# Expert weights in 8 KB runs, an earlier fourth split, and separate buffers for the first item of the expert loop

## The chip, the cores and the metric

One Trainium2 chip, one of its cores. The metric is the device time of one execution in microseconds (us), on the slowest core, which here is the only one. Of the kernel before three executions were timed.

## What is computed

One layer for two groups of tokens (256 prompt and 64 sample tokens, 1024 features, float32): modulation by a condition vector, one wide projection, retention and attention with forget gates, three output projections, a layer norm, a second modulation, and a mixture of 32 experts of which every token visits two. The change touches the second modulation and the mixture:

```python
h = x * (1 + sc2) + sh2                      # after the first layer norm
g_prob = softmax(h @ w_rg + b_rg)            # 4 groups, the best one is taken
e_logits = h @ w_re + b_re                   # 8 experts in the group, the best two
a, u = split(h[t] @ w_e_in[e], 2)            # w_e_in[e] is 1024 x 1024
y = (silu(a) * u) @ w_e_out[e] * gate        # w_e_out[e] is 512 x 1024
```

## The kernel before

The layer ahead of the experts streams 68 blocks of weights, 1 MB each, and ends near 575 us of the span. Then come the second modulation, the router and the sorting of tokens into items, and from about 622 us the loop of experts. An item is one expert with up to 64 token slots; there are 32 items in this run, and all 32 experts' weights are read, 6 MB for each.

**Numbers in two parts.** Products with weights run in TensorE's fp32r form on a high and a low part of each operand. ACT copies a block `raw` (128 x 2048) to its rounded high part `whi` (`item_hi`, L997), DVE subtracts it from the block to get the low part `wlo` (`item_lo`, L1618). There are six raw buffers and three pairs of parts. The last of an item's six blocks is not split: PE reads it from its raw buffer in plain float32 (`product_plain`, L2075).

**One item.** `item_products(e)` on PE multiplies the transposed tokens `xT` with blocks 0 and 1 (L2063 for the high parts, L2067 for the low ones), transposes the hidden rows of the item before (`hidden_T`, L2082), multiplies with blocks 2 and 3, transposes the tokens of the next item (`x_transpose`, L2054), and ends with the second product of the item before: block 4 split, block 5 plain. Its first product goes to banks 0 and 1 of PSUM, the second to banks 2 and 3.

**The order of the work** is written out by hand, one list for each engine. On ACT: split 0, silu of the item before, split 1, `y_low`, split 2, `hidden_high` (L1014), splits 3 and 4, `au_low` (L1018), `x_high` (L1002). On DVE: low part 0, `hidden` (L1631), low 1, `y_sum` (L1642), low 2, `hidden_low` (L1635), lows 3 and 4, `au_sum` (L1627), `x_low` (L1622). A split into slot 0 or 1 for blocks 3 and 4 waits until PE has used blocks 0 and 1 of the same item (`split_free`). SP sends the six blocks in order (L571), each when its raw buffer is free: after its low part is made, or for block 5 after PE has used it. POOL gathers the tokens of an item (L744, L767) and scatters its result (L750, L777).

**Runs of the transfers.** Partition p of a block takes rows p and 128 + p of 256 rows, each 4 KB long, so a block is 256 runs of 4 KB. Token features lie on the partitions in the same order.

**The first item.** Item 0 uses the same `xT` and the same banks 0 and 1 as all others. So the tokens of item 1 are transposed after item 0's four products (`x_transpose(1)`), ACT brings them to `xT` behind `au_low`, and item 1's first product waits for `au_drained`. The last block of item 0 has extra buffers (`xhi`, `xlo`).

**Modulation and router.** `modulated(t)` makes the rows `h2` of 128 (or 64) tokens with two instructions (L1215, L1217); PE transposes them and multiplies with the router weights `wr` (`logits`, L2013). POOL loads `wr` (L722, L723) and stores `h2` for the gathers (L729, L731).

## Time and profile before

| | us |
|---|---|
| median of three executions | 1201.11 |
| lowest, highest | 1198.50, 1202.01 |
| the profiled execution's own time | 1200.38 |
| its span, first to last instruction | 1198.5 |
| mean granted clock of TensorE | 0.942 of full |

| stretch of the span | what it is |
|---|---|
| 0 to 575 us | the layer ahead of the experts |
| 575 to 622 us | second modulation, router, sorting |
| 622 to 649 us | items 0 and 1 |
| 649 to 1141 us | thirty items in a steady rhythm |
| 1141 to 1198.5 us | last product, gathering of the results, second layer norm |

How to read it: the profile is one execution. For each engine it gives busy time, and for each instruction what ended the idle time before it. PE is TensorE, PEld its weight loads, DVE VectorE, ACT ScalarE, POOL GpSimd, SP the engine that only sends transfers. A matmul's duration in the rows overlaps that of the next one; what it costs is seen from start to start. DMA share is how busy the core's 16 DMA engines were; it can pass 1, since a packet's time includes waiting.

### The profile page before, as it was taken

The page shows a single profiled execution, that of the slowest core. Times are in us where ns is not written, and L with a number is a line of the kernel's source. Part 1 is how long each engine was busy: PE and PEld are TensorE (multiplying, and loading weights), DVE is VectorE, ACT ScalarE, POOL GpSimd, SP SyncE. Part 2 cuts the span into 40 slices and gives each one's busy share as a digit, 9 for nine tenths or more (in the row PEclk, how much of TensorE's full clock was granted, in tenths as well). Part 3 has the DMA queues.
Part 4 walks back from the last instruction along what each step waited for, and adds up shares of the span by engine and source line. Part 5 has one row for each costly group of instructions (what it writes and reads, how often), then busy time and mean ns, then how long its engine had stood idle before and what let it go on. Part 6 is the DMA issues. An engine that isn't in the chain of part 4 may idle for free.

```text
span 1198.5 us, 13069 instructions
## 1 busy us (share of the span) xinstructions
PE 1030.9 (86%) x4460; PEld 718.5 (60%) x4460; DVE 882.7 (74%) x942; ACT 638.0 (53%) x646; POOL 198.2 (17%) x179
## 2 busy tenths in 40 slices
PE   4798789899999999999748999999999999999940
PEld 2365567587777677677636566566566566565630
DVE  3768884396433544565857999999999999899967
ACT  3654324223323344433407777777777777777832
POOL 1250671010001000002001221121221121221210
PEclk8788899999999999999758999999999999999975
DMA  9777544265123324336428999999999999999922
GB/s 325 268 264 239 200 151 158 80 214 181 53 80 124 123 79 150 106 141 202 133 88 297 403 394 389 388 392 396 396 393 397 396 395 391 383 392 392 397 76 99
DMA packets 102698, 303.41 MB, mean 253 GB/s; under 512 B 10770, under 2 KB 10818, under 8 KB 102150
## 3 DMA queue, kind: packets, MB, share of 16 engines
q1 hardware_dynamic: 92888, 282.75, 63.5%
q0 software_dynamic: 9776, 20.21, 5.4%
q8 instruction: 21, 0.34, 0.1%
q14 instruction: 13, 0.11, 0.0%
HBM read 299.99 MB, written 14.73 MB: 263 GB/s over the span
## 4 chain that ended last, share of the span: by engine, by line
PE 68%; DVE 15%; ACT 6%; DMA 4%; issue 4%; POOL 2%; SPq 0%; ACTq 0%; POOLq 0%; DVEq 0%
PE banks L2067 10%; PE banks L1753 10%; PE banks L1764 10%; PE banks L2075 8%; PE banks L2063 8%; PE banks L1755 6%; DVE w_lo L1618 6%; ACT w_hi L997 5%; DVE w_lo L1081 3%; PE banks L2054 2%; PE banks L2082 1%; DMA w_raw<-in_w_ada 1%; PE banks L1814 1%; DMA scratch_y<-y_item,slot_row_now 1%; POOL h_hi L644 1%
## 5 line engine op out<-in xcount | busy, mean ns | idle before, releaser
L1618 DVE TENSOR_TENSOR w_lo<-w_raw,w_hi 128x2048 fp32r<-128x2048 f32 x157 | 356.0, 2284 | 47.3 <-ACT w_hi L997 47.3
L997 ACT ACTIVATE w_hi<-w_raw 128x2048 fp32r<-128x2048 f32 x157 | 295.5, 1903 | 7.4 <-PE banks L2067 7.2
L1081 DVE TENSOR_TENSOR w_lo<-w_raw,w_hi 128x2048 fp32r<-128x2048 f32 x71 | 170.3, 2413 | 69.8 <-ACT w_hi L815 69.7
L815 ACT ACTIVATE w_hi<-w_raw 128x2048 fp32r<-128x2048 f32 x71 | 134.8, 1910 | 133.2 <-PE banks L1764 108.4
L2067 PE MATMUL banks<-w_lo,xT_item 128*128 128x512 f32 x508 | 147.5, 412 | 41.3 <-DVE w_lo L1618 41.3
L2063 PE MATMUL banks<-w_hi,xT_item 128*128 128x512 f32 x508 | 157.1, 432 | 4.1 <-DVE xT_item L1622 3.6
L1753 PE MATMUL banks<-w_hi,h_hi 128*128 128x512 f32 x384 | 141.0, 408 | 7.9 <-DVE mod_rows L1237 5.2
L2067 PEld LDWEIGHTS banks<-w_lo,xT_item 128*128 128x128 f32 x508 | 91.9, 190 | 85.9 <-DVE w_lo L1618 68.0
L2063 PEld LDWEIGHTS banks<-w_hi,xT_item 128*128 128x128 f32 x508 | 94.6, 192 | 39.3 <-issue 14.3
L2075 PE MATMUL banks<-w_raw,hiddenT 128*128 128x512 f32 x248 | 111.5, 592 | 0.0
L1764 PE MATMUL banks<-w_lo,h_hi 128*128 128x512 f32 x384 | 108.5, 404 | 3.3 <-DVE w_lo L1081 3.3
L1755 PE MATMUL banks<-w_hi,h_lo 128*128 128x512 f32 x256 | 102.2, 399 | 0.0
L750 POOL DMA_INDIRECT scratch_y<-y_item,slot_row x29 | 63.2, 2179 | 234.1 <-DVE y_item L1642 217.6
L1753 PEld LDWEIGHTS banks<-w_hi,h_hi 128*128 128x128 f32 x384 | 72.0, 189 | 27.3 <-issue 6.0
L1764 PEld LDWEIGHTS banks<-w_lo,h_hi 128*128 128x128 f32 x384 | 69.8, 189 | 20.9 <-DVE w_lo L1081 3.7
L2075 PEld LDWEIGHTS banks<-w_raw,hiddenT 128*128 128x128 f32 x248 | 47.2, 190 | 47.4 <-issue 44.5
L1018 ACT ACTIVATE au_low<-banks 64x1024 f32<-64x1024 f32 x32 | 32.8, 1025 | 58.0 <-PE banks L2067 58.0
L744 POOL DMA_INDIRECT x_item<-scratch_h,slot_token x32 | 30.2, 943 | 195.8 <-PE banks L2054 174.9
L1755 PEld LDWEIGHTS banks<-w_hi,h_lo 128*128 128x128 f32 x256 | 48.7, 190 | 10.4
L1415 DVE TENSOR_REDUCE neg_max<-banks 64x1 f32<-64x192 f32 x16 | 5.6, 350 | 62.4 <-PE banks L1935 62.4
L1010 ACT ACTIVATE y_low<-banks 64x1024 f32<-64x1024 f32 x32 | 32.8, 1025 | 25.5 <-PE banks L2075 17.4
L1804 PE MATMUL banks<-w_lo,c_parts 128*64 128x512 f32 x96 | 34.4, 492 | 13.5 <-DVE w_lo L1081 13.1
(431 smaller groups left out, 1444.3 us busy)
## 6 DMA issues: line engine op xcount, KB each, us to landing
w_raw<-in_w_e_in SPq DMA_DIRECT2D x128, 1024.0 KB, 7.3
w_raw<-in_w_e_out SPq DMA_DIRECT2D x64, 1024.0 KB, 6.6
w_raw<-in_w_in SPq DMA_DIRECT2D x32, 1024.0 KB, 7.9
w_raw<-in_w_ada SPq DMA_DIRECT2D x24, 1024.0 KB, 7.7
bias_rows<-in_b_in SPq DMA_DIRECT2D x16, 256.0 KB, 4.3
w_raw<-in_w_ret_proj SPq DMA_DIRECT2D x4, 1024.0 KB, 10.6
w_raw<-in_w_fox_proj SPq DMA_DIRECT2D x4, 1024.0 KB, 11.6
w_raw<-in_w_o SPq DMA_DIRECT2D x4, 1024.0 KB, 5.0
```

Of the source, the lines that this page charges most:

```text
L750: nc.gpsimd.indirect_dma_start(yd[:, :], bass.IndirectOffsetOnAxis(ap=row[:, e:e + 1], axis=0), ySb[:].rearrange("p a b -> p (a b)"), None ...
L815: nc.scalar.activation(whi[n % NSPL][:], raw[n % NRAW][:], ACT.Copy).then_inc(hi_done, 1)
L997: nc.scalar.activation(whi[ss][:], raw[j][:], ACT.Copy).then_inc(hi_done, 1)
L1081: V.tensor_tensor(wlo[n % NSPL][:], raw[n % NRAW][:], whi[n % NSPL][:].bitcast(F32), ALU.subtract).then_inc(lo_done, 1)
L1618: V.tensor_tensor(wlo[ss][:], raw[j][:], whi[ss][:].bitcast(F32), ALU.subtract).then_inc(lo_done, 1)
L1753: mm(b[:, :], H[:, k, cols], whi[n % NSPL][:, kk, :], start=(k == 0), stop=False)
L1755: mm(b[:, :], L[:, k, cols], whi[n % NSPL][:, kk, :], start=False, stop=False)
L1764: last = mm(b[:, :], H[:, 4 * s + kk, P * t:P * t + P], wlo[n % NSPL][:, kk, :], start=False, stop=(s == 1 and kk == 3))
L1804: last = mm(b[0:64, :], cst[:, 4 * s + kk, :], wlo[n % NSPL][:, kk, :], start=False, stop=(s == 1 and kk == 3))
L2063: mm(bank[b0 + half], X[:, k0 + kk, :], split_h[ss][:, 2 * kk + half, :], start=(first and kk == 0), stop=False)
L2067: last = mm(bank[b0 + half], X[:, k0 + kk, :], split_l[ss][:, 2 * kk + half, :], start=False, stop=(final and kk == 1))
L2075: last = mm(bank[b0 + half], X[:, k0 + kk, :].bitcast(F32), raw[rs][:, 2 * kk + half, :], start=False, stop=(kk == 1))
```

## The change

**Rows of the weights.** Partition p of a block now takes rows 2p and 2p + 1 of 256 rows. They lie side by side in memory, so a block is 128 runs of 8 KB. To match, feature 256j + 2p + i has to stand in the place 256j + 128i + p. `modulated` writes `h2` in that order, with four instructions in place of two, each reading every second element; `hidden` writes the hidden rows so, in one instruction that reads every second element; the router weights are loaded in that order by four transfers in place of two, and two waits count 96 in place of 64.

**Order of the fourth split.** On ACT split 3 comes ahead of `hidden_high`, on DVE low part 3 ahead of `hidden_low`, in every item.

**First item.** Item 0 has its own `xT0` and banks 6 and 7. Item 1's tokens are transposed after item 0's second product, brought to `xT` ahead of `au_low`, and item 1's first product no longer waits for `au_drained`. PE waits for the drained banks 6 and 7 before item 0.

**POOL** waits for item 0's four products before it sends the six transfers for the tail (L783 to L788).

```diff
+    xT0 = at("xT_first", [P, KD, 2 * SLOTS], F32R, 73728)
...
-    w_in_e = i["w_e_in"][0].rearrange("e (k p) n -> e p k n", p=P)
-    w_out_e = i["w_e_out"][0].rearrange("e (k p) n -> e p k n", p=P)
+    w_in_e = i["w_e_in"][0].rearrange("e (j p i) n -> e j p (i n)", p=P, i=2)
+    w_out_e = i["w_e_out"][0].rearrange("e (j p i) n -> e j p (i n)", p=P, i=2)
...
+    FIRST_BANK = 6
 
     def sub(e, j):
 
...
                 sp.dma_start(bf_col[:], i["b_in"][0, FGATE:FGATE + FH].rearrange("(p a) -> p a", a=1)).then_inc(wf_in, 16)
 
         def pair(r):
-            return r[:].rearrange("p a b -> p (a b)").rearrange("p (k n) -> p k n", k=2)
+            return r[:].rearrange("p a b -> p (a b)")
 
         for n in range(4):
             s = N0 + n
             sp.wait_ge(lo_done, s - NRAW + 1)
-            sp.dma_start(pair(raw[s % NRAW]), w_in_e[0, :, 2 * n:2 * n + 2, :]).then_inc(raw_landed[s % NRAW], 16)
+            sp.dma_start(pair(raw[s % NRAW]), w_in_e[0, n]).then_inc(raw_landed[s % NRAW], 16)
 
         def raw_free(e, j):
 
...
             for j in range(6):
-                src = (w_in_e[expert, :, 2 * j:2 * j + 2, :] if j < 4
-                       else w_out_e[before, :, 2 * (j - 4):2 * (j - 4) + 2, :])
+                src = w_in_e[expert, j] if j < 4 else w_out_e[before, j - 4]
                 if not isinstance(e, int):
-                    src = src.rearrange("e p k n -> (e p) k n")
+                    src = src.rearrange("e p n -> (e p) n")
                 raw_free(e, j)
                 sp.dma_start(pair(raw[j]), src).then_inc(raw_landed[j], 16)
...
-        pool.dma_start(wr[:, :, 0:NG], i["w_rg"][0].rearrange("(k p) n -> p k n", p=P)).then_inc(wr_in, 16)
-        pool.dma_start(wr[:, :, NG:], i["w_re"][0].rearrange("(k p) n -> p k n", p=P)).then_inc(wr_in, 16)
+        wr4 = wr[:].rearrange("p (j i) n -> p j i n", i=2)
+        for half in range(2):
+            pool.dma_start(wr4[:, :, half, 0:NG], i["w_rg"][0].rearrange("(j p i) n -> p j i n", p=P, i=2)[:, :, half, :]).then_inc(wr_in, 16)
+            pool.dma_start(wr4[:, :, half, NG:], i["w_re"][0].rearrange("(j p i) n -> p j i n", p=P, i=2)[:, :, half, :]).then_inc(wr_in, 16)
         pool.dma_start(br[:, 0:NG], bcast(i["b_rg"][0], P)).then_inc(wr_in, 16)
         pool.dma_start(br[:, NG:], bcast(i["b_re"][0], P)).then_inc(wr_in, 16)
 
...
         gather_item(1)
         gather_item(2)
+        pool.wait_ge(used, N0 + 4)
         pool.dma_start(g2p[:], bcast(md[0, 3 * D:4 * D], P)).then_inc(tail_in, 16)
         pool.dma_start(g2s[:], bcast(md[1, 3 * D:4 * D], DEC)).then_inc(tail_in, 16)
         pool.dma_start(l1w[:], bcast(i["ln1_w"][0], P)).then_inc(tail_in, 16)
...
             act.wait_ge(x_trans, e + 1)
-            nc.scalar.activation(xT[:, :, 0:SLOTS], bank[4][:, :].rearrange("p (k c) -> p k c", k=KD), ACT.Copy).then_inc(x_hi, 1)
+            dst = xT0 if isinstance(e, int) and e == 0 else xT
+            nc.scalar.activation(dst[:, :, 0:SLOTS], bank[4][:, :].rearrange("p (k c) -> p k c", k=KD), ACT.Copy).then_inc(x_hi, 1)
 
...
             act.wait_ge(used, after + 1)
-            nc.scalar.activation(auLo[:], banks[SLOTS:P, 0:2, :], ACT.Copy).then_inc(au_lo, 1)
+            b0 = FIRST_BANK if isinstance(after, int) and after == N0 + 3 else 0
+            nc.scalar.activation(auLo[:], banks[SLOTS:P, b0:b0 + 2, :], ACT.Copy).then_inc(au_lo, 1)
 
         x_high(0)
         item_hi(1, 0)
+        x_high(1)
         au_low(N0 + 3)
-        x_high(1)
 
         def item(e, second):
             if not (isinstance(e, int) and e == 1):
...
                 y_low(e - 2, sub(e - 1, 5))
             item_hi(e, 2)
+            item_hi(e, 3)
             hidden_high(e - 1)
-            item_hi(e, 3)
             item_hi(e, 4)
             au_low(sub(e, 3))
             x_high(e + 1)
...
-            st(V.scalar_tensor_tensor(ht, xt, mv[0:rows, t, 0:1], m2[0:rows, 1, :], ALU.subtract, ALU.mult))
-            st.settle()
-            st(V.scalar_tensor_tensor(ht, ht, mv[0:rows, t, 1:2], m2[0:rows, 0, :], ALU.mult, ALU.add), h2_ready)
+            for i in range(2):
+                hv = ht.rearrange("r (j i p) -> r j i p", i=2, p=P)[:, :, i, :]
+                st(V.scalar_tensor_tensor(hv, xt.rearrange("r (j p i) -> r j p i", i=2, p=P)[:, :, :, i], mv[0:rows, t, 0:1],
+                                          m2[0:rows, 1, :].rearrange("r (j p i) -> r j p i", i=2, p=P)[:, :, :, i], ALU.subtract, ALU.mult))
+            st.settle()
+            for i in range(2):
+                hv = ht.rearrange("r (j i p) -> r j i p", i=2, p=P)[:, :, i, :]
+                st(V.scalar_tensor_tensor(hv, hv, mv[0:rows, t, 1:2], m2[0:rows, 0, :].rearrange("r (j p i) -> r j p i", i=2, p=P)[:, :, :, i],
+                                          ALU.mult, ALU.add), h2_ready if i else None)
 
         def evac_ada(j):
...
             dve.wait_ge(x_hi, e + 1)
-            V.tensor_tensor(xT[:, :, SLOTS:], bank[4][:, :].rearrange("p (k c) -> p k c", k=KD),
-                            xT[:, :, 0:SLOTS].bitcast(F32), ALU.subtract).then_inc(x_split, 1)
+            dst = xT0 if isinstance(e, int) and e == 0 else xT
+            V.tensor_tensor(dst[:, :, SLOTS:], bank[4][:, :].rearrange("p (k c) -> p k c", k=KD),
+                            dst[:, :, 0:SLOTS].bitcast(F32), ALU.subtract).then_inc(x_split, 1)
 
...
-            V.tensor_tensor(auS[:], banks[0:SLOTS, 0:2, :], auLo[:], ALU.add).then_inc(au_drained, 1)
+            b0 = FIRST_BANK if isinstance(e, int) and e == 0 else 0
+            V.tensor_tensor(auS[:], banks[0:SLOTS, b0:b0 + 2, :], auLo[:], ALU.add).then_inc(au_drained, 1)
 
         def hidden(e):
             dve.wait_ge(silu_ok, e + 1)
-            V.tensor_tensor(hid[:], aA[:], auS[:, 1, :], ALU.mult).then_inc(hid_ok, 1)
+            V.tensor_tensor(hid[:].rearrange("r (j i p) -> r j i p", i=2, p=P), aA[:].rearrange("r (j p i) -> r j i p", i=2, p=P),
+                            auS[:, 1, :].rearrange("r (j p i) -> r j i p", i=2, p=P), ALU.mult).then_inc(hid_ok, 1)
 
         def hidden_low(e):
...
         dve.wait_ge(hi_done, N0 + 4)
         V.tensor_tensor(xlo[:], raw[(N0 + 3) % NRAW][:], xhi[:].bitcast(F32), ALU.subtract).then_inc(lo_done, 1)
         x_low(0)
+        x_low(1)
         item_lo(1, 0)
         au_sum(0)
-        x_low(1)
 
...
                 y_sum(e - 2, third)
             item_lo(e, 2)
+            item_lo(e, 3)
             hidden_low(e - 1)
-            item_lo(e, 3)
             item_lo(e, 4)
...
         x_transpose(0)
         pe.wait_ge(x_split, 1)
         pe.wait_ge(slt_done, 1)
+        pe.wait_ge(*use["pos"][3])
+        pe.wait_ge(*use["cnt"][3])
         for n in range(4):
-            product(N0 + n, (N0 + n) % NSPL if n < 3 else NSPL, 0, xT, 2 * n, n == 0, n == 3)
-        x_transpose(1)
+            product(N0 + n, (N0 + n) % NSPL if n < 3 else NSPL, FIRST_BANK, xT0, 2 * n, n == 0, n == 3)
+            if n == 1:
+                x_transpose(1)
 
         def item_products(e, second):
             pe.wait_ge(x_split, e + 1)
-            pe.wait_ge(au_drained, e)
+            if not (isinstance(e, int) and e == 1):
+                pe.wait_ge(au_drained, e)
             for j in range(2):
                 product(split_sub(e, j), SPLIT_SLOT[j], 0, xT, 2 * j, j == 0, False)
```

## Rows read from the trace of the kernel before

**Rows 1.** Windows: us, busy us of each engine, clock, DMA share, GB/s; the loop

```profile
700.00:1100.00 400.00, 367.76 (x1507) 242.61 (x1506) 366.73 (x245) 306.52 (x245) 75.10 (x49) 1.00 1.01 392
```

**Rows 2.** Waits of ACT in the loop, and issue to landing of two items' weights

```profile
ACT w_hi L997 <- PE banks L2067: 0.4, 1, 0.4
...
w_raw<-in_w_e_in SPq DMA_DIRECT2D x8, 1024.0 KB, 7.5
```

**Rows 3.** Timeline of one item, DVE: start, us, instruction, idle before and its releaser

```profile
907.09 4.49 DVE L1618 TENSOR_TENSOR w_lo<-w_raw,w_hi 128x2048 fp32r<-128x2048 f32 x2 [0.56 <-ACT w_hi L997]
...
914.14 2.29 DVE L1618 TENSOR_TENSOR w_lo<-w_raw,w_hi 128x2048 fp32r<-128x2048 f32 x1 [0.61 <-ACT w_hi L997]
...
920.29 2.27 DVE L1618 TENSOR_TENSOR w_lo<-w_raw,w_hi 128x2048 fp32r<-128x2048 f32 x1
922.49 0.41 DVE L1635 TENSOR_TENSOR hiddenT<-banks,hiddenT 128x256 fp32r<-128x256 f32 x1
923.46 2.29 DVE L1618 TENSOR_TENSOR w_lo<-w_raw,w_hi 128x2048 fp32r<-128x2048 f32 x1 [0.56 <-ACT w_hi L997]
```

**Rows 4.** The same item's timeline, ACT and PE

```profile
912.21 1.91 ACT L997 ACTIVATE w_hi<-w_raw 128x2048 fp32r<-128x2048 f32 x1
...
917.89 1.91 ACT L997 ACTIVATE w_hi<-w_raw 128x2048 fp32r<-128x2048 f32 x1
921.24 0.39 ACT L1014 ACTIVATE hiddenT<-banks 128x256 fp32r<-128x256 f32 x1 [1.44 <-PE banks L2082]
921.52 3.71 ACT L997 ACTIVATE w_hi<-w_raw 128x2048 fp32r<-128x2048 f32 x2
...
909.44 1.19 PE L2067 MATMUL banks<-w_lo,xT_item 128*128 128x512 f32 x4 [1.06 <-DVE w_lo L1618]
...
917.69 1.10 PE L2067 MATMUL banks<-w_lo,xT_item 128*128 128x512 f32 x4
```

**Rows 5.** Token transposes that bound thirty items, from the PE timeline

```profile
648.55 0.62 PE L2054 MATMUL banks<-pack,x_item 64*128 64x64 f32 x5
...
1141.29 0.87 PE L2054 MATMUL banks<-pack,x_item 64*128 64x64 f32 x9
```

**Rows 6.** DMA of 900 to 934 us, then windows with 2 KB, 4 KB and 8 KB runs

```profile
DMA packets 3747, 13.43 MB, mean 395 GB/s; under 512 B 469, under 2 KB 469, under 8 KB 3746
...
20.00:30.00 10.00, 7.17 (x20) 3.53 (x20) 5.95 (x4) 3.82 (x2) 0.00 (x0) 0.66 1.05 387
904.00:916.00 12.00, 10.65 (x47) 6.82 (x46) 10.70 (x7) 9.30 (x8) 3.13 (x2) 1.00 1.03 412
...
1167.00:1171.00 4.00, 0.00 (x0) 0.00 (x0) 0.52 (x3) 1.15 (x1) 0.00 (x0) 0.50 1.01 426
```

**Rows 7.** Window of the loop in which the granted clock fell

```profile
1026.00:1029.00 3.00, 3.00 (x8) 2.33 (x9) 2.26 (x4) 2.98 (x4) 0.94 (x1) 0.52 1.03 416
```

**Rows 8.** DVE groups by shape: hidden, the modulation, two reductions

```profile
L1631 DVE TENSOR_TENSOR hidden<-a_silu,au_sum 64x512 f32<-64x512 f32 x32 | 21.6, 676 | 0.8 <-ACT a_silu L1006 0.8
...
L1217 DVE SCALAR_TENSOR_TENSOR h<-h,ln_mean_var,mod_prompt 128x1024 f32<-128x1024 f32 x2 | 2.6, 1285 | 0.1
...
L1515 DVE TENSOR_REDUCE expert_logits<-expert_masked 128x24 f32<-128x96 f32 x1 | 0.3, 322 | 0.0
...
L1554 DVE TENSOR_REDUCE extra_items<-count_cmp 128x32 f32<-128x128 f32 x1 | 0.3, 285 | 0.0
```

**Rows 9.** Timeline of items 0 and 1, ACT

```profile
632.13 1.02 ACT L1018 ACTIVATE au_low<-banks 64x1024 f32<-64x1024 f32 x1 [1.73 <-PE banks L2067]
633.18 0.60 ACT L1002 ACTIVATE xT_item<-banks 128x512 fp32r<-128x512 f32 x1
...
635.62 3.70 ACT L997 ACTIVATE w_hi<-w_raw 128x2048 fp32r<-128x2048 f32 x2
```

**Rows 10.** POOL's loads of the router weights

```profile
564.18 0.94 POOL L722 DMA_DIRECT2D w_router<-in_w_rg  x1 [8.57 <-PE banks L1764]
...
587.53 3.60 PE L2013 MATMUL banks<-w_router,h2T 128*128 128x36 f32 x16 [0.78 <-ACT h2T L972]
```

6 lines of the change are left out of this document (3 added, 3 removed).

## The prediction

> **What bounds the kernel now.** I read the loop first, since thirty items of it take 492.74 us of the span: the token transposes at both ends of it start at 648.55 and 1141.29 [rows 5], so an item takes 16.42 us in the mean. The windows then show three resources near their end at once: over 400 us PE is busy for 92%, DVE for 92%, and the DMA engines for all of it at 392 GB/s [rows 1]. A busy share doesn't say which one sets the pace, so I look at waits. ACT, the first to touch a block of weights, never waits for a transfer in the loop; its one wait ahead of a split is 0.4 us for PE [rows 2]. So the transfers keep up, and DMA is full because SP sends early. What sets the pace is a ring of hand-overs. Follow DVE: it idles twice in an item, 0.61 us ahead of low part 0 and 0.56 us ahead of low part 3, both times for a split on ACT [rows 3]. ACT makes split 3 late because it stands behind `hidden_high`, for which ACT sat idle for 1.44 us until PE had transposed the hidden rows [rows 4]. PE in turn waits 1.06 us for low part 3 [rows 4]. From low part 3 to the next low part 3 an item takes 923.46 - 907.09 = 16.37 us [rows 3].
>
> **The fourth split.** The ring in two parts. From low part 3 to low part 0 it is 914.14 - 907.09 = 7.05 us [rows 3]: low part 3, PE's last four matmuls at 909.44, `au_low`, `x_high`, split 0 at 912.21 for 1.91 us [rows 4]. Nothing in it moves. `hidden_low` now lies between low parts 3 and 4, which ends 0.41 us later; low part 3 itself is not moved by that, and of the 0.61 us that DVE idles ahead of low part 0 some 0.1 goes, since `au_sum` now comes behind low part 4 and not behind `au_low`. It still waits for split 0.
>
> From low part 0 to low part 3 it was 923.46 - 914.14 = 9.32 us. Low part 3 now stands where `hidden_low` starts, right behind low part 2, at 922.49 [rows 3]. That takes off 0.97 us: 0.56 of idle and 0.41 of `hidden_low`, which lands where DVE had idle time. The ring is then 922.49 - 907.09 = 15.40 us.
>
> What could be late next, each by the same timeline. Split 3 follows split 2: 917.89 + 2 x 1.86 = 921.6 (two splits in a row take 3.71), 0.9 us ahead of its low part [rows 4]. It needs the slot of block 0, which PE leaves at 917.69 + 1.10 = 918.79, 0.9 us before ACT asks for it at 919.7 [rows 4]. `hidden_high` moves from 921.24 to 921.6, split 4 behind it to about 921.9 and ends by 923.8; low part 4 wants it at 922.49 + 2.20 + 0.33 = 925.0, so 1.2 us are spare. `hidden_low` starts behind low part 3, near 924.7, and PE wants it after its token transpose, two microseconds after low part 3: spare. On PE the pause of 1.06 us ahead of low part 3 shrinks to about 0.1.
>
> Thirty items: 492.74 - 30 x 15.40 = 30.7 us. Of this 29.1 are the ring and 1.6 the one item above 16.37: from 1026 to 1029 PE's clock was granted at 0.52 of full speed, that is its lower level of 1.2 GHz, where the loop as a whole shows 1.00, the higher one of 2.4 GHz [rows 1, 7]. PE had not done less before it than in every item: it had made its pause ahead of low part 3. With shorter pauses I take this one as gone; if it stays, 1.6 us are to be added.
>
> **8 KB runs.** An item moves 13.43 MB x 16.37 / 34 = 6.47 MB [rows 6]. Where DMA is full, 2 KB runs went at 387 GB/s, 4 KB runs, which this loop has, at 412, and the one transfer with 8 KB runs, the gathering of results at the end, at 426 over 4 us [rows 6]. The steps 387 and 412 give the same by a fixed cost for each run: on one of 16 engines 2 KB takes 84.7 ns and 4 KB 159.1 ns, so another 4 KB 148.8, and 8 KB in 308 ns on 16 engines are 426 GB/s. An item then needs 6.47 / 0.426 = 15.19 us of DMA, under the 15.40 of the ring; with 4 KB runs it would be 15.70, over it. So the longer runs are worth nothing alone (DMA is hidden now), and make room for the other part. I take 15.19, with 15.70 as the upper end. Landing: low part 0 is made at 916.43 and the next split 0 starts 16.37 after 912.21, at 928.58; a block lands 7.5 us after it is sent [rows 2]. At most 4.6 us are spare for SP's own delay, 3.7 after the change: enough.
>
> The Trainium skill (DMA: Bandwidth & Descriptors, Why small descriptors are slow) puts a packet's own cost at some 3 beats beside one for each 32 bytes. By it 8 KB runs would be 1.2% faster than 4 KB ones, 417 GB/s and 15.5 us for an item, 0.1 us above the ring. The trace shows 6.5% between 2 and 4 KB where that rule gives 2.3%, so it doesn't agree.
>
> **Reading every second element.** `hidden` (676 ns) lies on the ring, between low parts 0 and 1 [rows 8]. No row reads 512 elements at this step. From below the cost is nothing. From above I take the one row that reads at a wide step, a reduction of 96 elements over steps of 8: 322 ns, where 128 elements in a row took 285 [rows 8]. An element costs 1.19 ns (1285 - 676 ns for 512 more, the two shapes of [rows 8]), so 96 in a row would take 247; the step costs 75 ns, 0.78 for an element, and on 512 that is 0.40 us for an item. I take nothing, since the step is two and that row's is eight, and keep 0.40 for the range. The modulation pays the same on its 1285 ns instructions [rows 8], of which only the first tokens' two stand before anything can hide them: split in four they add some 0.1 us, for two more starts, and 4 x 0.4 = 1.6 us at the upper end.
>
> The Trainium skill (SBUF — State Buffer, Door 1) says that SBUF is read in lines of 16 bytes and that two hits on a line are enough for full speed. Every second float32 gives two hits, every eighth one; the row with the step of eight agrees with it. By this rule `hidden` keeps its 676 ns.
>
> **The first item.** The transpose of item 1's tokens now lies between item 0's products: 9 small matmuls of 0.87 us together [rows 5], so `au_low` moves from 632.13 to about 633.0. `x_high` of 0.60 us no longer stands between it and the table load that silu needs, and split 1 of item 1, which leads the chain from there, moves by 0.87 - 0.60 from 635.62 to 635.9 [rows 9]. PE starts item 1 some 2 us earlier and then waits for that split. I take 0.3 us lost; if PE's clock happens to stay up, up to 3 us are won. POOL's new wait has the tail's six loads and the gather for item 3 queued behind it; the loads are used after the loop, and the gather waits for a later transpose of PE anyway. The two added loads of router weights cost POOL 2 x 0.94 us near 566; with the 7.5 us to land of [rows 2] they are in by 576, and PE wants them at 587.5 [rows 10]. The new waits for banks 6 and 7 are for work long done.
>
> **The sum.** -30.7 + 0.3 + 0.1 = -30.3 us. Against the profiled execution's 1200.38 that is 1170.1; the median of 1201.11 is 0.7 above it, so 1170.8.
>
> **Rivals.**
> - DMA becomes the bound, because 8 KB runs bring nothing: 30 x (16.42 - 15.70) = 21.7, and some 2 us more from buffers that run dry at the end; 1177. For it: only 4 us of trace have 8 KB runs, and they have no gathers beside them. Against it: the two other run lengths point to the same 426. A rate in between gives a time in between.
> - The step of two costs 0.40 us in `hidden`, and 1.6 us in the modulation: 30.3 - 12.0 - 1.6 = 16.7; 1184.4. Only one row, with another step and another instruction, speaks for it.
> - Slower: 8 KB runs go at a lower rate beside gathers, and ACT waits for landings. The point is 6.47 / 16.42 = 394 GB/s. At the 387 of 2 KB runs an item takes 16.72 us; 30 x 0.3 = 9 us more, 1210. Against it: the rate rises with the run in all three rows.
> - The order does not do what it says: the wait for PE only moves from split 3 to split 4 and on to low part 4. It needs more than the 1.2 us that I find spare, plus 0.97; about 1200.
>
> **How the numbers follow.** The ring 0.60, with its own range of 1167 to 1175 (the clock either way, the start); DMA as the bound 0.20; the step of two 0.10; no change 0.04; slower 0.05; better than the ring's range 0.01. The range from 1166 to 1185 holds all but the last three, and I keep these ends since DMA and the step can each be paid in part. A measurement of this kernel can tell about 0.3%, 3.6 us, from no change. Faster 0.91, within 0.3% 0.04, slower 0.05.
>
> **What the profile will show.** Right: low part 3 to low part 3 in 15.4 us; `hidden_low` behind low part 3 with no idle before it; DVE's only idle time in an item ahead of low part 0; PE's pause ahead of low part 3 gone; packets of 8 KB with DMA near 420 GB/s; `hidden` at 676 ns. If splits on ACT show a wait for `w_raw` transfers, DMA is the bound. If `hidden` shows about 1.08 us, the step is paid. If `hidden` is as it was, no transfer is waited for and an item still takes over 16 us, my ring is wrong.

## The result and the profile after

The changed kernel takes 1186.56 us (median of four runs, 1186.50 to 1187.36) against 1201.56 (four runs, 1198.50 to 1205.24): a ratio of 0.9886, 95% interval 0.9856 to 0.9917. So it is faster, by 15.0 us, about half of the 30.3 that were forecast, and the time lies 1.6 us above the forecast's range. The profiled execution took 1186.54 us, its span is 1184.7, and the mean clock 0.944 of full.

Three token transposes of the changed kernel, from the PE timeline (start us, us, instruction), answer to [rows 5]; they open items 2, 10 and the last product. Under them stands the window of the loop that answers to [rows 1]:

```profile
651.40 0.87 PE L2069 MATMUL banks<-pack,x_item 64*128 64x64 f32 x9
775.15 0.87 PE L2069 MATMUL banks<-pack,x_item 64*128 64x64 f32 x9
1127.48 0.87 PE L2069 MATMUL banks<-pack,x_item 64*128 64x64 f32 x9
...
700.00:1100.00 400.00, 382.04 (x1559) 248.44 (x1558) 374.46 (x253) 327.94 (x252) 113.00 (x51) 1.00 1.01 406
```

Thirty items now take 1127.48 - 651.40 = 476.08 us, 16.66 less than the 492.74 of before. But they are of two kinds. The first eight take (775.15 - 651.40) / 8 = 15.47 us, six of them 15.38 to 15.40, which is the ring of 15.40 that was forecast. The other 22 take (1127.48 - 775.15) / 22 = 16.01 us. Both kinds can be read in DVE's timeline, first an item at 682, then one at 907:

```profile
686.05 2.29 DVE L1630 TENSOR_TENSOR w_lo<-w_raw,w_hi 128x2048 fp32r<-128x2048 f32 x1 [0.51 <-ACT w_hi L1001]
688.25 0.68 DVE L1645 TENSOR_TENSOR hidden<-a_silu,au_sum 64x512 f32<-64x512 f32 x1
...
691.06 1.21 DVE L1657 TENSOR_TENSOR y_item<-banks,y_low 64x1024 f32<-64x1024 f32 x1
692.19 4.48 DVE L1630 TENSOR_TENSOR w_lo<-w_raw,w_hi 128x2048 fp32r<-128x2048 f32 x2
696.59 0.41 DVE L1650 TENSOR_TENSOR hiddenT<-banks,hiddenT 128x256 fp32r<-128x256 f32 x1
...
907.43 2.29 DVE L1630 TENSOR_TENSOR w_lo<-w_raw,w_hi 128x2048 fp32r<-128x2048 f32 x1 [1.35 <-ACT w_hi L1001]
...
923.58 2.29 DVE L1630 TENSOR_TENSOR w_lo<-w_raw,w_hi 128x2048 fp32r<-128x2048 f32 x1 [1.20 <-ACT w_hi L1001]
```

Against [rows 3], low part 3 stands behind low part 2 (the `x2` at 692.19), `hidden_low` follows with no idle time, and the only idle time of the item at 682 is the one ahead of low part 0. In the later item this same idle time has grown from 0.51 to 1.35 us. DVE waits there for split 0, and ACT's timeline says what split 0 waits for:

```profile
904.16 0.60 ACT L1007 ACTIVATE xT_item<-banks 128x512 fp32r<-128x512 f32 x1
905.49 1.91 ACT L1001 ACTIVATE w_hi<-w_raw 128x2048 fp32r<-128x2048 f32 x1 [0.73 <-DMA w_raw<-in_w_e_in]
...
911.54 1.91 ACT L1001 ACTIVATE w_hi<-w_raw 128x2048 fp32r<-128x2048 f32 x1 [0.63 <-DMA w_raw<-in_w_e_in]
```

Now the loop's waits (engine and line, what it waited for: us in total, times, longest) and the landing of the weights from 900 to 934 us (KB each, us from issue to landing), which answer to [rows 2]:

```profile
ACT w_hi L1001 <- DMA w_raw<-in_w_e_in: 26.8, 57, 1.0
DVE w_lo L1630 <- ACT w_hi L1001: 25.0, 29, 1.4
...
w_raw<-in_w_e_in SPq DMA_DIRECT2D x8, 1024.0 KB, 11.3
```

Before, ACT waited for no transfer of weights in the loop and a block landed 7.5 us after it was sent. Now it waits 57 times for one, and a block takes 11.3 us. So the ring was shortened as forecast, and from about the eighth item on the transfers set the pace, at 16.0 us for an item where the forecast had 15.19. The change from one kind to the other shows in the time from issue to landing, here from 650 to 680 us and from 740 to 770 us:

```profile
w_raw<-in_w_e_in SPq DMA_DIRECT2D x7, 1024.0 KB, 7.6
...
w_raw<-in_w_e_in SPq DMA_DIRECT2D x8, 1024.0 KB, 10.8
```

The transfers of 900 to 934 us in 40 equal slices, and two windows (us, busy us of each engine, clock, DMA share, GB/s), answer to [rows 6]:

```profile
GB/s 414 424 395 381 410 424 434 443 414 414 414 280 318 405 424 405 443 414 424 414 443 405 419 400 434 376 453 434 414 424 313 304 318 434 443 376 443 443 424 376
DMA packets 2152, 13.75 MB, mean 404 GB/s; under 512 B 422, under 2 KB 422, under 8 KB 526
...
912.00:919.00 7.00, 6.01 (x26) 3.93 (x25) 7.00 (x6) 5.68 (x4) 1.96 (x1) 1.00 1.01 419
909.00:911.50 2.50, 2.50 (x11) 1.88 (x10) 2.50 (x3) 1.89 (x2) 0.00 (x0) 1.00 1.02 326
```

The packets fell from 3747 to 2152, so the 8 KB runs are there, and in most slices they go at 400 to 440 GB/s. But once per item the rate falls to about 300 for some 2.5 us, with the DMA engines as busy as before. POOL's timeline has the gather of an item's tokens at 904.65 and 920.97; it lands 7.3 us after it is sent. What these dips are is the question of the experiments.

### The profile page after: what moved, and what is told of

Its sections match the earlier page's. It is cut to its first block, busy times and chain, and to the rows that moved or that the text cites. A ratio compares the mean times of both kernels' runs of the same rounds, so it can differ in the third digit from the quotient of the medians.

```text
span 1184.7 us, 13078 instructions
## 1 busy us (share of the span) xinstructions
PE 1033.2 (87%) x4460; PEld 716.2 (60%) x4460; DVE 878.8 (74%) x948; ACT 651.5 (55%) x646; POOL 257.7 (22%) x181
## 4 chain that ended last, share of the span: by engine, by line
PE 47%; DVE 20%; DMA 15%; issue 10%; ACT 5%; POOL 2%; SPq 1%; ACTq 0%; POOLq 0%; DVEq 0%
PE banks L1768 10%; PE banks L1779 10%; DMA w_raw<-in_w_e_in 10%; DVE w_lo L1630 9%; PE banks L1770 7%; PE banks L2082 3%; ACT w_hi L1001 3%; PE banks L2090 3%; DVE w_lo L1087 3%; PE banks L2078 2%; DMA w_raw<-in_w_ada 1%; DVE y_item L1657 1%; PE banks L1829 1%; POOL h_hi L645 1%; DMA scratch_y<-y_item,slot_row 1%
## 5 line engine op out<-in xcount | busy, mean ns | idle before, releaser
L1001 ACT ACTIVATE w_hi<-w_raw 128x2048 fp32r<-128x2048 f32 x157 | 299.6, 1912 | 44.1 <-DMA w_raw<-in_w_e_in 28.9
L753 POOL DMA_INDIRECT scratch_y<-y_item,slot_row x29 | 113.8, 3925 | 238.7 <-DVE y_item L1657 221.2
L2078 PE MATMUL banks<-w_hi,xT_item 128*128 128x512 f32 x496 | 151.9, 428 | 2.9 <-ACT w_hi L1001 2.9
L2082 PEld LDWEIGHTS banks<-w_lo,xT_item 128*128 128x128 f32 x496 | 87.7, 190 | 72.1 <-DVE w_lo L1630 57.2
L2078 PEld LDWEIGHTS banks<-w_hi,xT_item 128*128 128x128 f32 x496 | 91.6, 190 | 36.5 <-issue 14.3
L1819 PE MATMUL banks<-w_lo,c_parts 128*64 128x512 f32 x96 | 32.1, 464 | 15.6 <-DVE w_lo L1087 15.1
L1816 PE MATMUL banks<-w_hi,c_parts 128*64 128x512 f32 x96 | 32.9, 475 | 13.3 <-ACT w_hi L819 13.3
```

Of the source, the lines that this page charges most:

```text
L753: nc.gpsimd.indirect_dma_start(yd[:, :], bass.IndirectOffsetOnAxis(ap=row[:, e:e + 1], axis=0), ySb[:].rearrange("p a b -> p (a b)"), None ...
L1001: nc.scalar.activation(whi[ss][:], raw[j][:], ACT.Copy).then_inc(hi_done, 1)
L1816: mm(b[0:64, :], cst[:, 4 * s + kk, :], whi[n % NSPL][:, kk, :], start=(s == 0 and kk == 0), stop=False)
L2078: mm(bank[b0 + half], X[:, k0 + kk, :], split_h[ss][:, 2 * kk + half, :], start=(first and kk == 0), stop=False)
L2082: last = mm(bank[b0 + half], X[:, k0 + kk, :], split_l[ss][:, 2 * kk + half, :], start=False, stop=(final and kk == 1))
```

## The experiments

An item's time below is from one token transpose to the next. For each run I compare it with the changed kernel's two values, 15.39 (ring) and 16.02 us (mean of the last twenty).

**The new order alone**, 4 KB runs, first item as before:

```diff
             item_hi(e, 2)
+            item_hi(e, 3)
             hidden_high(e - 1)
-            item_hi(e, 3)
...
             item_lo(e, 2)
+            item_lo(e, 3)
             hidden_low(e - 1)
-            item_lo(e, 3)
```

> The kernel before with split 3 ahead of hidden_high and low part 3 ahead of hidden_low, nothing else: 4 KB runs, the first item as before. Theory A (DMA sets the pace, and longer runs raise its rate): the first items take 15.4 us, then ACT waits for transfers and an item takes 16.2 to 16.4 us; 1194 to 1200 us. Theory B (DMA sets the pace, run length does not matter): items settle at 16.0 us as in the changed kernel; 1186 to 1188 us. My forecast's own rates (4 KB at 412 GB/s): 15.7 us for an item, 1178 us.

Measured: 1193.22 us, ratio 0.9931 (0.9908 to 0.9954). The loop's first two items take 16.14 and 17.04 us, the next two 15.46 and 15.41, then they settle near 16.3 (the last twenty have a mean of 16.35). The loop's window and, of 800 to 1100 us, ACT's wait:

```profile
700.00:1100.00 400.00, 375.02 (x1523) 242.41 (x1522) 366.86 (x246) 322.13 (x246) 87.83 (x49) 1.00 1.02 398
...
ACT w_hi L997 <- DMA w_raw<-in_w_e_in: 23.0, 37, 1.0
```

The order works by itself, and with 4 KB runs the transfers allow 398 GB/s and 16.35 us. That is nearly the old ring of 16.37, so before the change two bounds lay on top of each other. Not all of the 8.6 us is the order's. The loop of the profiled execution gains 4.2 us (488.52 against 492.74). Another 2.8 lie in items 0 and 1, which take 26.12 us from the first to the third token transpose where they took 28.92. The granted clock is what differs there: it fell near 640 us in the kernel before, and not in this execution. The windows from 640 to 649 us, before and here:

```profile
640.00:649.00 9.00, 9.00 (x30) 6.54 (x31) 6.69 (x4) 4.33 (x4) 0.00 (x0) 0.62 1.02 350
```

```profile
640.00:649.00 9.00, 9.00 (x45) 6.58 (x45) 8.33 (x6) 6.51 (x6) 0.98 (x1) 1.00 1.02 351
```

In the changed kernel it fell there too (0.65 in the same window), so this gain does not come with the order.

**The longer runs alone**, with the old order and the old first item:

```diff
-            item_hi(e, 3)
             hidden_high(e - 1)
+            item_hi(e, 3)
...
-            item_lo(e, 3)
             hidden_low(e - 1)
+            item_lo(e, 3)
```

(against the changed kernel; its first item is undone too, as in the run on the first item below)

> The changed kernel with the old order of the fourth split and the old first item; only the 8 KB runs and the permuted rows are left. All theories: the old ring sets the pace with 16.37 us for an item, ACT never waits for a transfer; 1199 to 1202 us. If the ring was not what held the kernel before and DMA was, it drops to 16.0 us and 1188 us.

Measured: 1202.62 us, ratio 1.0012 (0.9984 to 1.0040). Items take 16.37 us, and ACT has no wait for a transfer. The window of its loop and the landing of its weights:

```profile
700.00:1100.00 400.00, 368.05 (x1497) 242.86 (x1496) 363.94 (x243) 304.08 (x243) 76.39 (x49) 0.99 0.98 390
...
w_raw<-in_w_e_in SPq DMA_DIRECT2D x8, 1024.0 KB, 7.0
```

The runs are worth nothing alone, as forecast. The DMA share is 0.98 here, where before it was 1.01 with 4 KB runs and the same 16.37 us.

**What the transfers allow.** The changed kernel with half of each low part left out (the subtraction of blocks 0 to 4 covers half a block), once with 8 KB and once with 4 KB runs. That takes some 5 us of DVE from an item, so DVE no longer sets the pace:

```diff
-            V.tensor_tensor(wlo[ss][:], raw[j][:], whi[ss][:].bitcast(F32), ALU.subtract).then_inc(lo_done, 1)
+            V.tensor_tensor(wlo[ss][:, 0:2, :], raw[j][:, 0:2, :], whi[ss][:, 0:2, :].bitcast(F32), ALU.subtract).then_inc(lo_done, 1)
```

> The changed kernel with every low part of the loop's blocks made for half of the block only (the other half keeps old numbers, so part of the products is left wrong): DVE's ring falls well under 15 us and the pace is that of the transfers alone. Theories A and B: 16.0 us for an item, about 404 GB/s, ACT waiting for weights in every item, near 1184 to 1187 us. My forecast's rate of 426 GB/s: 15.2 us for an item, 1163 us.

> The same with the 4 KB runs and the old order of features: half low parts, pace of the transfers alone. Theory A: 16.2 to 16.4 us for an item, 395 to 399 GB/s. Theory B: 16.0 us. My forecast's rate of 412 GB/s: 15.7 us.

Measured: 1183.60 us with 8 KB runs, ratio 0.9848 (0.9783 to 0.9913), and 1192.99 with 4 KB, ratio 0.9927 (0.9893 to 0.9962). Both begin with items of 14.5 us: three with 8 KB runs, two with 4 KB. Then 8 KB runs give 16.00 and 4 KB runs 16.35 us (last twenty). The two windows of the loop, 8 KB first:

```profile
700.00:1100.00 400.00, 388.97 (x1554) 245.41 (x1553) 247.90 (x251) 328.36 (x251) 47.94 (x50) 1.00 1.01 407
```

```profile
700.00:1100.00 400.00, 385.99 (x1519) 237.70 (x1517) 242.80 (x245) 321.73 (x245) 50.84 (x49) 1.00 1.02 398
```

DVE, the third engine of the window, has 248 busy us instead of 374, and an item takes what it takes in the changed kernel (16.00 against 16.02). That is the floor of the transfers. Doubling the run is worth 0.35 us in an item, 2.1%. The Trainium skill (DMA: Bandwidth & Descriptors, Why small descriptors are slow) has a fixed cost for each packet, from which an estimate of 1.2% follows for this step. These runs show more than that, and less than the 3.4% that the forecast took from short windows.

**Gathers that move nothing.** The row numbers of all gathers from item 1 on are out of range, so that they are sent and land but move no token. The items then work on item 0's tokens, with the same instructions:

```diff
-        st(V.tensor_copy(idx[:], slt[:, 0, :]), idx_ready)
+        st(V.tensor_scalar(idx[:, 1:], slt[:, 0, 1:], SKIP, None, ALU.add))
+        st(V.tensor_copy(idx[:, 0:1], slt[:, 0, 0:1]), idx_ready)
```

> The changed kernel with the gathers of items 1 and up pointed out of range, so that they move no token rows (all items then work on item 0's tokens; the output is not the layer's). Once in an item the rate of all transfers falls to 326 GB/s for 2.5 us while the gather's rows move. Theory C (the gather slows all transfers, beyond its own 0.08 MB): the dips are gone, the floor falls to about 6.37 MB at 419 GB/s = 15.2 us, the ring of 15.4 us sets the pace, ACT's waits for transfers vanish; 1172 to 1176 us. Theory D (the dip has another cause that only falls together with the gather): 15.8 us for an item by the bytes saved, 1181 to 1184 us.

Measured: 1174.01 us, ratio 0.9761 (0.9718 to 0.9804). The first item of the loop takes 15.69 us and the other 29 take 15.38 to 15.40 to the end, ACT waits for no transfer in the loop, and a block lands in 8.3 us. The DMA share of the loop is still 1.01, at 414 GB/s, though no engine waits for a transfer. The transfers of 900 to 934 us, as above:

```profile
GB/s 414 434 424 424 386 443 419 400 434 386 366 405 424 395 405 434 443 414 414 424 453 424 395 443 400 410 434 405 357 405 453 395 414 424 443 424 434 395 443 424
DMA packets 2236, 14.17 MB, mean 417 GB/s; under 512 B 482, under 2 KB 482, under 8 KB 532
```

The dips are gone, while the scatters of results are still there. So the dips belong to the rows that the gathers bring, and they are what keeps the changed kernel from its ring: 16.02 - 15.39 = 0.63 us for an item at the least. A gather brings 20 rows of 4 KB in the mean (640 visits in 32 items), 0.08 MB, which at 417 GB/s would be 0.2 us. The changed kernel's window of the dip gives the same size: 2.5 x (419 - 326) / 419 = 0.55 us. Without them the kernel is 2.4% faster than the one before, 28.7 us of 1202.8 (1174.01 / 0.9761), close to the 30.3 forecast.

**Where the rows come from.** Gathers from item 1 on read the same row numbers of another tensor, `w_o`; the items work on those rows:

```diff
...
-            nc.gpsimd.indirect_dma_start(xg[:], None, h2d[:, :], bass.IndirectOffsetOnAxis(ap=idx1[:, 0:1], axis=0),
+            nc.gpsimd.indirect_dma_start(xg[:], None, other[:, :], bass.IndirectOffsetOnAxis(ap=idx1[:, 0:1], axis=0),
```

> The changed kernel with the gathers of items 1 and up reading the same row numbers of another tensor of 4 KB rows (w_o) in place of the stored h2 (output not the layer's). If it matters where the rows lie in memory, the dips go and an item takes 15.4 to 15.6 us. If the dip belongs to the gather as such, whatever it reads: 16.0 us for an item, 1186 to 1188 us.

Measured: 1185.42 us, ratio 0.9856 (0.9812 to 0.9900), items of 16.05 us, and the dips as before. It makes no difference which of these two tensors the rows come from.

**Where the rows go.** The tokens of an item are spread, with a step of four partitions. 20 tokens then lie on partitions 0 to 31 instead of 0 to 19 (slots from 32 on go to partitions 32 to 63 in the same way); all is computed:

```diff
-        st(V.tensor_tensor(oh_s[:], io_s, cp6.unsqueeze(2).to_broadcast([P, 6, SLOTS]), ALU.is_equal))
+        for g in range(2):
+            cols = slice(32 * g, 32 * g + 32)
+            st(V.tensor_tensor(oh_s[:, :, cols].rearrange("p q (a b) -> p q b a", b=4),
+                               iota[:, cols].rearrange("p (b a) -> p b a", a=8).unsqueeze(1).to_broadcast([P, 6, 4, 8]),
+                               cp6.unsqueeze(2).unsqueeze(3).to_broadcast([P, 6, 4, 8]), ALU.is_equal))
```

> The changed kernel with the slots of an item permuted over the 64 partitions, so that the first 8 tokens lie 4 partitions apart instead of side by side; everything is still computed. Theory E (the gather's rows fall on few partitions, whose share of the engines' paths is loaded more than the others): the dips get shorter, an item takes 15.7 to 15.9 us, 1178 to 1184 us. Otherwise 16.0 us, 1186 to 1188 us.

Measured: 1186.02 us, ratio 0.9852 (0.9815 to 0.9888); items of 15.91 us instead of 16.02. In the time no difference to the changed kernel can be told. The items are 0.1 us shorter, a little more than the changed kernel's own traces differ (15.98 to 16.02 in three of them). The crowding is only lessened by this run and not removed; what 0.1 us means is taken up below.

**The first item as before**, with the new runs and the new order:

```diff
-            dst = xT0 if isinstance(e, int) and e == 0 else xT
+            dst = xT
...
-        x_high(1)
         au_low(N0 + 3)
+        x_high(1)
...
-            product(N0 + n, (N0 + n) % NSPL if n < 3 else NSPL, FIRST_BANK, xT0, 2 * n, n == 0, n == 3)
-            if n == 1:
-                x_transpose(1)
+            product(N0 + n, (N0 + n) % NSPL if n < 3 else NSPL, 0, xT, 2 * n, n == 0, n == 3)
+        x_transpose(1)
```

> The changed kernel with the first item as before (xT, banks 0 and 1, item 1's tokens transposed behind item 0, no new wait on POOL). My forecast and all theories: items as in the changed kernel, 15.4 us for the first and 16.0 us later; the first item's own part is worth 0.3 us or less either way, unless TensorE's clock differs; 1184 to 1188 us.

Measured: 1186.51 us, ratio 0.9876 (0.9838 to 0.9914), the time of the changed kernel. Item 0's own buffers bring nothing and cost nothing that can be told. From the first to the third token transpose it takes 28.8 us, against 29.1 with the buffers and 28.9 before.

**A plain load in the gather's place.** From item 1 on, POOL sends a plain load of stored tokens 0 to 19 (in a second run 0 to 63) instead of the gather, at the same place; all those items work on these tokens:

```diff
...
-            nc.gpsimd.indirect_dma_start(xg[:], None, h2d[:, :], bass.IndirectOffsetOnAxis(ap=idx1[:, 0:1], axis=0),
-                                         bounds_check=T - 1, oob_is_err=False).then_inc(x_landed, 16)
+            pool.dma_start(xg[0:20, :], h2d[0:20, :]).then_inc(x_landed, 16)
```

> The changed kernel, with the gather of every item from item 1 on replaced by one plain load of the rows 0 to 19 of the stored tokens into the same buffer, on the same queue and at the same place. 20 rows of 4 KB are what a gather moves in the mean (640 token visits over 32 items), to the same partitions 0 to 19. All these items then work on the same 20 tokens; the sequence of instructions on the other engines is unchanged. Theory F, it is the indirect form that costs (a row address for every packet, made on the way): the items after the first seven fall to 15.4 to 15.5 us and the time to about 1174 to 1176 us, as with gathers that moved no rows (1174.0). Theory G, it is any small load in packets of 4 KB into few partitions beside the stream of weights: the items stay near 16.0 us and the time near 1186. A plain load might be cut into other packets than a gather; the packets show it.

> As the run before, with rows 0 to 63 in the plain load: 0.26 MB on 64 partitions, 0.18 MB more than 20 rows. At the 407 GB/s of the stream that alone is 0.45 us of transfer time for an item. Theory F: items of 15.4 (the ring) plus at most that, since the ring has 0.2 to 0.4 us of spare transfer time; 15.5 to 15.9 us, 1176 to 1184. Theory G: if the cost goes with the number of small packets, it is three times that of 20 rows: 16.0 + 1.2 = over 17 us, 1220 or more; if it goes with the load as an event, some 16.3 us, 1196.

Measured: 1186.87 us with 20 rows, ratio 0.9863 (0.9806 to 0.9919), items of 15.93 us; 1218.35 with 64 rows, ratio 1.0124 (1.0067 to 1.0182), items of 17.07. The transfers of 900 to 934 us with 64 rows:

```profile
GB/s 405 395 448 434 414 424 424 361 251 284 299 405 405 443 414 414 414 453 405 424 405 414 443 395 443 434 410 294 299 260 308 424 424 405 434 424 424 405 443 405
...
x_item<-scratch_h POOLq DMA_DIRECT2D x2, 256.0 KB, 7.4
```

The indirect form is not the cause: 20 rows by a plain load cost about as much as a gather. By these two, 64 rows make an item at least 17.07 - 15.39 = 1.68 us longer, 26 ns a row, and 20 rows 15.93 - 15.39 = 0.54 us, 27 ns a row, where 4 KB in the stream of weights take 4096 / 417 = 10 ns. That looked like a price for each row.

**The same loads on ACT's queue**, sent behind `x_high`:

```diff
...
-            nc.gpsimd.indirect_dma_start(xg[:], None, h2d[:, :], bass.IndirectOffsetOnAxis(ap=idx1[:, 0:1], axis=0),
-                                         bounds_check=T - 1, oob_is_err=False).then_inc(x_landed, 16)
...
             nc.scalar.activation(dst[:, :, 0:SLOTS], bank[4][:, :].rearrange("p (k c) -> p k c", k=KD), ACT.Copy).then_inc(x_hi, 1)
+            act.dma_start(xg[0:20, :], scratch["h2"][0:20, :]).then_inc(x_land2, 16)
```

(against the changed kernel)

> The run with 20 plain rows, with the load sent by ACT behind the copy of the transposed tokens (`x_high`) instead of by POOL after the same transpose: the same bytes, the same 20 partitions and nearly the same moment, but on ACT's queue, which the hardware serves, and not on POOL's. The send itself stands on ACT's way to split 0, so the ring grows by what it costs ACT; I take 0.1 us (a send of POOL's stands at 0.94 us in the rows, as the upper end). All items work on the same 20 tokens. Theory H, POOL's queue is what makes small packets dear: items after the first eight at the ring, 15.4 to 15.6 us, and 1175 to 1180 us. Theory G, it is the small packets themselves, whoever sends them: near 16.0 us, 1187, as with POOL's load (1186.9).

> The same with 64 rows, 0.26 MB. By POOL's queue the items stood at 17.07 us and the time was 1218. Theory H: a load of 0.26 MB at the stream's rate adds 0.45 us over that of 20 rows, so items of 15.5 to 15.9 us and 1177 to 1187 us. Theory G: as by POOL's queue, items near 17.1 us, 1218.

Measured: 1187.77 us with 20 rows, ratio 0.9858 (0.9752 to 0.9965), last items of 15.91 us, and 1217.50 with 64 rows, ratio 1.0105 (0.9997 to 1.0213), items of 16.97. POOL's queue is not the cause either.

**Is it the rows or where they land?** Two plain loads by POOL from item 3 on, into a spare buffer: 4 rows into partitions 0 to 3, or 64 rows into partitions 32 to 95. Items 1 and 2 load 20 rows, and all items work on those tokens:

```diff
...
-            nc.gpsimd.indirect_dma_start(xg[:], None, h2d[:, :], bass.IndirectOffsetOnAxis(ap=idx1[:, 0:1], axis=0),
-                                         bounds_check=T - 1, oob_is_err=False).then_inc(x_landed, 16)
+            pool.dma_start(xd[0:4, :], h2d[0:4, :]).then_inc(x_landed, 16)
```

> The changed kernel; in place of the gathers from item 3 on POOL sends a plain load of 4 stored rows, 16 KB, into partitions 0 to 3 of a spare buffer (items 1 and 2 load 20 rows). All items from the first on work on the same 20 tokens. Theory R, a price for each row (27 ns by the loads of 20 and 64 rows): 4 rows cost 0.1 us, items at the ring, 15.4 us, and some 1174 us. Theory S, the busiest group of partitions sets the price: partition p belongs to group (p / 4) mod 8 of the lower or upper 64, so partitions 0 to 3 are one group and get 4 rows, as each of the five groups of a load of 20 rows does. The stream's 417 GB/s are 26 GB/s for each of 16 groups; 16 KB more in one of them take 0.63 us. So 4 rows cost what 20 cost: items of 15.9 to 16.0 us, 1186 us. In between would say that the hold-up is shared. The Trainium skill (SBUF — State Buffer, Door 1: The DMA port swizzle) gives this grouping, 16 ports of 8 partitions; the trace so far has nothing against it, since the loads of 20 and of 64 rows cost 0.54 and 1.68 us.

> As the run before, with 64 rows into partitions 32 to 95 of the spare buffer. The same load into partitions 0 to 63 gave items of 17.07 us and 1218 us. Theory R: the same again, 17.0 to 17.1 us and 1218. Theory S: partitions 32 to 63 are eight groups, 64 to 95 the other eight, so each of 16 groups gets 4 rows where partitions 0 to 63 gave each of eight groups 8 rows: the cost is that of one group's 4 rows, 0.63 us, and since all groups are loaded alike it is also just that of the bytes, 0.26 MB at 417 GB/s: items of 15.9 to 16.1 us and 1184 to 1190 us. By the Trainium skill (SBUF — State Buffer, Door 1: The DMA port swizzle) partitions 0 to 63 reach only 8 of 16 ports and 32 to 95 all of them.

Measured: 4 rows 1182.20 us, ratio 0.9833 (0.9787 to 0.9879), items of 15.86 us; 64 rows 1185.38 us, ratio 0.9860 (0.9817 to 0.9902), items of 15.88. The transfers of 900 to 934 us, first with 4 rows (busy tenths of the DMA engines and GB/s in 40 slices), then with 64:

```profile
DMA  9999999899999989999999999999999999899999
GB/s 395 434 434 443 414 395 434 357 453 453 405 405 424 424 308 386 405 424 395 434 414 453 405 405 395 453 386 424 443 386 424 414 347 308 347 366 376 395 424 434
```

```profile
GB/s 434 405 434 414 400 439 424 414 434 405 424 443 395 434 376 395 386 434 453 414 395 434 434 434 395 434 414 434 386 434 453 395 424 414 424 376 434 424 434 405
DMA packets 2172, 14.22 MB, mean 418 GB/s; under 512 B 347, under 2 KB 347, under 8 KB 525
```

A price for each row is out. Against the ring of 15.39, so at the least, 4 rows cost 0.47 us of an item, 20 cost 0.54, and 64 cost 0.49 or 1.68, by where they land. With 64 rows over partitions 32 to 95 there is no dip, and the engines move 418 GB/s in the mean; by this that load costs its bytes (0.26 MB, 0.63 us at 417 GB/s) and no more. With 4 rows in partitions 0 to 3, 16 KB in all, there are dips (308, then 347, 308 and 347 GB/s), and the three slices in which the DMA engines are not fully busy have 357, 308 and 347 GB/s. So for plain loads the cost goes with the rows in the busiest of 16 groups of partitions: 4, 4 and 4 rows in it at 0.47 to 0.54 us, 8 rows at 1.68. A fixed price for any load that brings rows would give the first three too, but neither the 1.68 us nor the missing dip. The forecast for 4 rows was 0.63; for 8 rows the same sum gives 1.26, and the rest of the 1.68 is not explained. The two loads of 64 rows differ in their buffer as well (the spare one against that of the tokens), which was not tried apart; in neither run does an engine wait for the load in the loop. It would fit that a block of weights lands only when its last part has, so that what one group takes on top holds up the whole stream; no view shows the groups one by one. The Trainium skill gives this grouping (SBUF — State Buffer, Door 1: The DMA port swizzle): 16 ports, partitions 0 to 63 reach only 8 of them, and partitions 32 to 95 all. These two runs agree with it. It also says (DMA: Bandwidth & Descriptors, The descriptor swizzle) that in a transfer to all 128 partitions each DMA engine serves one port; whether here the port or its engine is the narrow place no run shows.

**The gather over 16 groups.** First the direct way, with everything computed. Slots go to partitions 0 to 31 and 64 to 95, so that 20 tokens put at most 2 rows in any group; the transposes become plain products with columns of the identity:

```diff
...
-    xg = at("x_item", [SLOTS, D], F32, 0)
+    xg = at("x_item", [96, D], F32, 0)
...
-                step = tr if k else mm
-                last = step(bank[4][:, SLOTS * k:SLOTS * k + SLOTS], xg[:, P * k:P * k + P], ident[0:SLOTS, 0:SLOTS])
+                step = mm
+                last = step(bank[4][:, SLOTS * k:SLOTS * k + SLOTS], xg[:, P * k:P * k + P],
+                            ident[0:96, :].rearrange("q (h x c w) -> q h x w c", h=2, x=2, c=8)[:, :, 0].rearrange("q h w c -> q w h c"))
```

> The changed kernel with everything computed, its gathers spread over all 16 groups of partitions: slot s of an item goes to partition 64h + 4c + w with s = 16w + 8h + c, so that the first 16 tokens go to 16 different groups and 20 tokens put at most 2 rows in any. The buffer has 96 partitions, the token transposes multiply with the matching columns of the identity, and a second small product makes the row numbers for 96 partitions (six matmuls and three instructions more ahead of the first item, some 0.7 us). Theory S: the busiest group gets 2 rows, 8 KB, where it got 4; the load costs 0.2 to 0.32 us of an item where it cost 0.63, and an item takes 15.6 to 15.75 us where it took 16.02; over 22 items 6 to 9 us less, and against the changed kernel 1178 to 1181 us. Theory R: items as before, 16.0, and 1187 to 1188 us. Against both: the gather has 96 row numbers instead of 64, and the transposes as plain products may take PE a little longer, 0.1 us an item on the ring.

> The changed kernel itself, on the same chip and in the same rounds as the run before, so that the two can be compared: 1186 to 1187 us, ratio 0.987 to 0.989.

Measured: 1203.35 us (the median of twelve, of which one took 2556.2), ratio 1.0013 (0.9994 to 1.0031), the loop's first item 16.73 us and all others 16.19; the changed kernel beside it 1183.97, ratio 0.9859 (0.9831 to 0.9887). ACT has no wait for a transfer in the loop; it waits for PE, whose transposes take 2 us where they took 0.87. PE's and ACT's timelines at one of them:

```profile
915.39 2.01 PE L2083 MATMUL banks<-pack,x_item 96*128 96x64 f32 x16
...
917.43 0.60 ACT L1009 ACTIVATE xT_item<-banks 128x512 fp32r<-128x512 f32 x1 [0.82 <-PE banks L2083]
```

Those 0.82 us lie on the ring: 15.39 + 0.82 = 16.21. So the run cannot show a gain, but it sets a limit. The transfers keep up with 16.19 us for an item, and from 900 to 934 us a block lands nearly as soon as in the kernel before (7.5 us):

```profile
w_raw<-in_w_e_in SPq DMA_DIRECT2D x8, 1024.0 KB, 7.8
```

With this gather their floor is thus 16.19 us or less.

Then with true transposes over 96 partitions, into banks 6 and 7, the first item as before the change, and the slots of the scatter spread as well:

```diff
...
-                last = step(bank[4][:, SLOTS * k:SLOTS * k + SLOTS], xg[:, P * k:P * k + P], ident[0:SLOTS, 0:SLOTS])
+                last = step(bank[6 + k // 4][:, P * (k % 4):P * (k % 4) + 96], xg[:, P * k:P * k + P], ident[0:96, 0:96])
```

> The changed kernel with the gathers over 16 groups of partitions and everything computed, as in e15, but with the transposes in transpose mode: 96 columns each, into banks 6 and 7, from which ACT and DVE read the 64 that hold slots. Since items use banks 6 and 7 so, the first item is done as before the change (worth nothing by e8). Ahead of the loop six small products and six DVE instructions more, some 1 us. The ring: eight transposes of 96 instead of 64 columns, of whose 0.87 us `au_low` (1.02) covers all; 0 to 0.3 us more, so 15.4 to 15.7 us. Theory S: the transfers need 15.6 to 15.75 us by the busiest group's 2 rows (0.2 to 0.32 us over the 15.4 that they need at most without rows), so items of 15.6 to 15.8, against 16.0 of the changed kernel, and 22 x 0.25 to 0.4 less 1 us: 1179 to 1183 where the changed kernel of the same rounds has 1184 to 1187. If ACT waits for transfers as before and an item takes 16.0, theory S has no use here. If ACT waits for PE ahead of `x_high`, the transposes are again the price.

> The changed kernel in the same rounds as the run before: 1184 to 1187 us, items of 15.38 to 15.40 and later 16.0 us.

Measured: 1197.68 us, ratio 0.9968 (0.9951 to 0.9986), beside 1185.82, ratio 0.9876 (0.9853 to 0.9899), of the changed kernel. The transposes take 0.94 us, and early items stand at 15.4 to 15.6 us, so the ring is short. But the last twenty take 16.38, more than the changed kernel's 16.01, and ACT waits for transfers more (700 to 1100 us); the rates of 900 to 934 us stand below:

```profile
ACT w_hi L1002 <- DMA w_raw<-in_w_e_in: 35.5, 52, 1.8
...
GB/s 318 337 357 328 376 424 386 434 443 434 386 424 381 434 429 424 410 347 309 328 313 376 357 395 424 414 424 443 414 386 429 429 414 434 434 424 424 333 362 366
```

The dips are longer, not shorter. With 2 rows in the busiest group the forecast was an item of 15.6 to 15.8 us, so here it fails, by some 0.6 us. The 16.38 cannot be the price of the spread gather alone, since the run before had the same gather and a floor of 16.19 or less. The two runs differ in the scatter's slots, the banks and the first item, and in that the transfers bind in one and the ring in the other; which of these counts was not tried.

The run with the step of four partitions does not speak against the groups. 20 tokens put 3 rows in the busiest of 8 groups there and not 4, which by the same sum takes 0.16 us off an item, and 0.11 was measured. So for gathers the groups are neither shown nor out. How a gather's rows are shared out among the DMA engines no view here shows, and this stays open. So does whether two loads per item, or a scatter that moves nothing, would change it; neither was tried. No version of these beats the changed kernel.

## Why the prediction was right in kind and twice too large

**Right: what bounds the kernel before.** The ring of hand-overs by way of low part 3 set the pace. Its length was forecast at 15.40 us from [rows 3], and the trace has 15.38 to 15.40 wherever transfers don't bind: in six early items of the changed kernel, and in 29 of thirty with gathers that move nothing. In the item at 682 us its signs are there: `hidden_low` at once behind low part 3, DVE's only idle time ahead of low part 0, and no pause of PE ahead of low part 3. But the ring was only just the longer of the two. The transfers need 16.35 us for an item in 4 KB runs, and the ring took 16.37; "so the transfers keep up" was true with 0.02 us to spare, which the prediction did not see. In the changed kernel the ring, to which the forecast gave 0.60, sets the pace for some eight items and the transfers for the other 22.

**Right: the runs alone are worth nothing**, and make room for the order: 0.35 us in an item once both are in.

**Wrong: the term for the transfers.** The step that failed is "an item then needs 6.47 / 0.426 = 15.19 us", and with it the upper end of 15.70 for 4 KB runs. The floors are 16.00 and 16.35 us. The bytes were right; the rates were read from windows of 12 and of 4 us in which the rate was high [rows 6]. The window of 12 us lay between two gathers, and that of 4 us stands behind the loop, where no tokens are gathered. Yet the same rows have 395 GB/s over 34 us, and [rows 1] 392 over 400 us at a DMA share of 1.01. At that mean an item needs 6.47 / 0.395 to 6.47 / 0.392, that is 16.4 to 16.5 us. This sum only gives the item's own time back, whatever bounds it. What hinted that it was the transfers' floor too is the share: with 8 KB runs and the old order, where the floor is 16.00 and the ring 16.37, it is 0.98. The hint is a weak one, since the share is also 1.01 with gathers that move nothing, where the ring sets the pace. What shows the floor is the run with the order alone (16.35), and the one with half low parts and 4 KB runs (16.35).

**What it makes of the sum.** Eight items at 15.47 and 22 at 16.01 are 476.1 us instead of 30 x 15.40 = 462.0: 14.1 us, nearly all of the 15.3 that are missing. That early items run at the ring is the buffers' doing. The transfers fall behind by about 0.6 us with each item, six to eight of them, and the forecast had 3.7 us spare between landing and use. In the trace the time from issue to landing grows from 7.6 us over 8.5 and 9.6 to 10.8 (windows of 30 us from 650 to 770 us), and is 11.3 near 900. With half low parts they fall behind by 1.5 us with each item, and only three items take 14.5 us, with DVE's shorter work.

**The rivals.** The first, DMA as the bound, with a chance of 0.20, was what happened, in kind: ACT waits for `w_raw` transfers, as it was to show. Its time of 1177 was too low, since it leaned on the same 15.70; with the floor of 16.00 it would have been 30 x (16.42 - 16.00) = 12.6 us off and about 1188. The range's end of 1185 came from the price of the step of two (1184.4), which was not paid, so that it came within 1.6 us of the measured time is luck. The third rival's point of 394 GB/s, at which nothing is gained, was nearer than the 426 of the forecast: with 4 KB runs the loop has 398, with 8 KB runs 406. That the order does nothing is out. So is the step of two in `hidden`:

```profile
L1645 DVE TENSOR_TENSOR hidden<-a_silu,au_sum 64x512 f32<-64x512 f32 x32 | 21.7, 677 | 0.7 <-ACT a_silu L1011 0.7
...
L1228 DVE SCALAR_TENSOR_TENSOR h<-h,ln_mean_var,mod_prompt 128x512 f32<-128x512 f32 x4 | 2.8, 749 | 0.1
L1223 DVE SCALAR_TENSOR_TENSOR h<-x,ln_mean_var,mod_prompt 128x512 f32<-128x512 f32 x4 | 2.8, 738 | 0.0
```

These are DVE's groups by shape (busy us, mean ns of one, idle before). `hidden` stays at 677 ns [rows 8: 676]. The rule of the Trainium skill (SBUF — State Buffer, Door 1), two hits on a line of 16 bytes are enough, agrees with it. The modulation's instructions are a little dearer: the same operation on the same shape without a step takes 681 and 692 ns in this trace (L1181, L1183), and they take 738 and 749, which that rule does not give. Two of each stand in front of the router and end 0.25 us later than before; the forecast was 0.1.

**The first item.** It takes 29.12 us from the first to the third token transpose against 28.92: 0.2 lost, forecast 0.3. The clock fell near 640 us in both; the up to 3 us for a clock that stays up came in two other runs, the order alone (26.12 us) and the last gather over 16 groups (25.87). The changed loop starts 2.85 us later in the profiled executions (651.40 against 648.55). Of this 2.4 us are there before anything that the change touches, a difference between executions: in another profiled execution of the changed kernel the loop starts at 647.56.

**The clock.** The one item in which the granted clock fell to its lower level of 1.2 GHz [rows 7] has no counterpart in the changed kernel's loop: none of its thirty items takes more than 16.52 us, and windows of 50 us from 700 to 1100 all show 1.00, the higher level of 2.4 GHz. That was forecast. The other traces bear it out. With the old order and 8 KB runs three items took 17.9 us, and the windows of 715 to 719, 749 to 753 and 1029 to 1032 us have 0.57, 0.57 and 0.55. With the new order it fell inside the loop only in the two runs with loads of 64 rows over partitions 0 to 63, whose items take 17 us and longer. Why it falls in some items and not in others like them stays open.

## What to carry to other kernels

Do not read the transfers' floor from the best window of a loop: whatever lowers the rate once in a period (here a load of 20 token rows, 0.6 us of 16, three times its bytes) is part of the floor. Where the DMA share stands at 1.0, take the mean rate over whole periods: the transfers need no more time than it gives, and may need just that. Whether they do, a run tells in which the other engines have less work, as with half low parts here. When a ring of hand-overs is to be shortened, put that floor beside it first, since the gain ends there. And a loop with several buffers runs for a while at the ring even when the transfers are slower, so compare its late items, not its early ones; the time from issue to landing tells which of the two regimes it is in.

## What was not expected of the hardware

- A plain load of 4 rows of 4 KB into partitions 0 to 3, 0.25% of an item's bytes, costs the stream of weights beside it 0.47 us of 16, about as much as one of 20 rows (0.54) or one of 64 rows over partitions 32 to 95 (0.49), all measured against the ring and so at the least. 64 rows over partitions 0 to 63 cost 1.68 us and make the kernel slower than before the change (1218.35 us).
- In the dips the rate of all transfers falls from 419 to 326 GB/s for some 2.5 us. Who sends the load (POOL's queue or ACT's), its form and which of two tensors it is read from make 0.1 us of difference in an item or less.
- The scatters of results, with as many rows, show no such dip.
- Without dips one core's DMA engines hold 417 to 418 GB/s over 34 us in 8 KB runs.
- Eight transposes of 96 instead of 64 columns take 0.94 instead of 0.87 us; the same work as plain products takes 2.01.
- An instruction of two operations (SCALAR_TENSOR_TENSOR, 128x512) that reads every second element takes 738 to 749 ns instead of 681 to 692, where one of a single operation (`hidden`, 64x512) pays nothing.
